# One gather of 8 KB rows per slot, into one ring of eight places, for the expert retrieval of a two-layer backbone

## The reference

```
q = (xc @ w_q).reshape(-1, 8, 2, 128)
s = einsum('chpq,hpnq->chpn', q, sub_keys)
s_top, i_top = top_k(s, 16)
cand = s_top[:, :, 0, :, None] + s_top[:, :, 1, None, :]      # 16 x 16 sums per head
best, j = top_k(cand, 16)
e = i_top[:, :, 0][j // 16] * 128 + i_top[:, :, 1][j % 16]     # one of 16384 experts
gate = softmax(best)
u = take(u_tab, e);  hid = gelu(einsum('cd,chkd->chk', xc, u))
vsel = take(v_tab, e)
out = einsum('chk,chkd->cd', gate * hid, vsel)
```

## Time and profile before

| | before |
|---|---|
| median of 3 runs | 9257.01 us |
| profiled execution, span | 9253.9 us |
| granted TensorE clock, mean | 0.894 of full speed |
| PE, DVE, ACT, POOL busy over the span | 79%, 50%, 19%, 35% |
| bytes of the gathers (queue 0) | 1342.34 MB in 368640 packets |
| gathers, U and V | 1280 and 1280 |
| median from issue to landing, U and V | 6.1 us, 6.2 us |

### The profile page before, as it was taken

How to read it: one execution, slowest core, us unless ns; L and a number is a source line. 1 busy time by engine, 2 the same in 40 slices (tenths; PEclk the granted TensorE clock), 3 DMA queues, 4 the chain that set the end, 5 groups by cost and what they waited for, 6 DMA issues and landing times. The chain is left out here.

```text
span 9253.9 us, 95340 instructions
## 1 busy us (share of the span) xinstructions
PE 7315.0 (79%) x31078; PEld 4507.4 (49%) x31078; DVE 4618.2 (50%) x10131; ACT 1801.1 (19%) x3910; POOL 3234.3 (35%) x3073
## 2 busy tenths in 40 slices
PE   6888888889867676776678888889898677666766
PEld 2777776745433222222237777777454322222322
DVE  1555544550375555555525554555304755555555
ACT  1232222210111111111112222221101111111111
POOL 0001001100027777777601100101000377777775
PEclk8999998999988888888889999999998888888888
DMA  3000000112139999999830000001111499999997
GB/s 136 16 9 9 9 9 10 30 35 60 42 107 372 349 366 352 350 363 347 317 131 9 9 9 9 13 14 30 39 52 49 171 367 349 347 357 346 368 336 283
DMA packets 627068, 1521.21 MB, mean 164 GB/s; under 512 B 56546, under 2 KB 285560, under 8 KB 626808
## 3 DMA queue, kind: packets, MB, share of 16 engines
q0 software_dynamic: 368640, 1342.34, 39.0%
q1 hardware_dynamic: 257600, 174.74, 6.2%
q10 hardware_dynamic: 568, 0.22, 0.0%
HBM read 1513.43 MB, written 3.67 MB: 164 GB/s over the span
## 5 line engine op out<-in xcount | busy, mean ns | idle before, releaser
L1793 PE MATMUL ps<-arena 128*128 128x512 f32 x5120 | 2622.3, 671 | 1118.9 <-ACT arena L1686 1116.8
L1793 PEld LDWEIGHTS ps<-arena 128*128 128x128 f32 x5120 | 1075.0, 215 | 2667.7 <-ACT arena L1686 1356.4
L1732 DVE CUSTOM_DVE_ANT_0 arena<-arena 128x1024 f32<-128x1024 f32 x1280 | 1555.5, 1227 | 1314.6 <-DMA arena<-peer_u,arena 1295.0
L424 PE MATMUL ps<-h,w 128*128 128x512 f32 x5056 | 1474.9, 452 | 310.0 <-issue 131.1
L1667 POOL DMA_INDIRECT arena<-peer_v,arena x1280 | 1437.9, 1123 | 417.9 <-issue 339.7
L1667 POOL DMA_INDIRECT arena<-peer_u,arena x1280 | 1373.8, 1073 | 514.6 <-issue 329.3
L424 PEld LDWEIGHTS ps<-h,w 128*128 128x128 f32 x5056 | 811.9, 199 | 966.4 <-issue 903.1
L690 POOL MEMSET arena<- 64x640 f32 (+1 forms) x80 | 44.7, 559 | 1853.0 <-POOLq L83 1849.4
L1764 ACT ACTIVATE arena<-arena 128x4 f32<-128x4 f32 x320 | 66.1, 207 | 2949.1 <-DVEq L1737 2949.1
L966 DVE TENSOR_TENSOR arena<-ps,level 128x512 f32<-128x512 f32 (+1 forms) x480 | 273.3, 601 | 478.6 <-PE ps L757 476.2
L763 PE MATMUL ps<-arena 128*128 128x128 f32 x3200 | 409.4, 285 | 51.9 <-DVE arena L966 51.9
(11 more groups left out here) (288 smaller groups left out, 8761.6 us busy)
## 6 DMA issues: line engine op xcount, KB each, us to landing
w<-w_in SPq DMA_DIRECT2D x132, 512.0 KB, 4.0
arena<-ada_w SPq DMA_DIRECT2D x24, 2048.0 KB, 12.2
arena<-peer_u,arena POOLq DMA_INDIRECT x1280, 6.1
arena<-peer_v,arena POOLq DMA_INDIRECT x1280, 6.2
w<-peer_wq SPq DMA_DIRECT2D x32, 512.0 KB, 6.6
w<-w_a_out SPq DMA_DIRECT2D x16, 512.0 KB, 3.6
w<-w_out SPq DMA_DIRECT2D x16, 512.0 KB, 3.8
w<-w_b_out SPq DMA_DIRECT2D x16, 256.0 KB, 2.6
```

The lines of the kernel that those rows point to most:

```text
L424: mm = eng.matmul(psum[:, c0:c0 + n], m.w[:, slot, k, :], src[:, k, c0:c0 + n], start=(k == 0), stop=(k == KB - 1))
L1732: eng.tensor_tensor_reduce(ub[:, r, :], ub[:, r, :], hs, 1.0, 0.0, ALU.mult, ALU.add, hid[:, i:i + 1]).then_inc(u_free, 1)
L1793: mm = eng.matmul(m.bank(j), dg[:, r, :], vb[:, r, 512 * j:512 * j + 512], start=False, stop=False)
```

## The change

U and V of all experts are put beside each other into one table `peer_uv` before the launch: a row holds an expert's U and V, 2048 numbers, 8 KB. One gather per slot (1 MB) fetches both. The two rings of eight places of 4 KB become one ring of eight places of 8 KB, so the memory is the same. A place is freed by the slot's matmul, through one semaphore, `freed`. U's sum no longer frees anything; its semaphore (now `summed_u`) only tells DVE that four sums are written. DVE and PE wait for the same landing. The order written out on POOL, with its lead of four slots for U, gives way to a plain loop over the slots, and the row numbers of half a group are copied just ahead of slots 0 and 16.

```
-    ub, vb, dg = m.take(RING, D), m.take(RING, D), m.take(RING, P)
+    uv, dg = m.take(RING, 2 * D), m.take(RING, P)
...
-    def gather(eng, g, i, free, table, buf, landed):
-        off = bass.IndirectOffsetOnAxis(ap=stage.bitcast(U32)[:, i % GROUP:i % GROUP + 1], axis=0)
-        eng.wait_ge(free, g * GROUP + (i + 1))
+    def gather(eng, g, i):
+        if i % HALF == 0:
+            stage_rows(eng, g, i // HALF)
+        off = bass.IndirectOffsetOnAxis(ap=stage.bitcast(U32)[:, i:i + 1], axis=0)
+        eng.wait_ge(freed, g * GROUP + (i + 1))
         eng.sem_inc(asked, 1)
-        eng.indirect_dma_start(buf[:, i % RING, :], None, table, off).then_inc(landed[i % RING], 16)
...
+        eng.indirect_dma_start(uv[:, i % RING, :], None, table, off).then_inc(uv_in[i % RING], 16)
...
-            stage_rows(eng, 0, 0)
-            for i in range(LEAD):
-                gather_u(eng, 0, i)
-            with eng.Fori(0, TILES * GROUPS_T - 1) as g:
+            with eng.Fori(0, TILES * GROUPS_T) as g:
                 for i in range(GROUP):
-                    if i == HALF - LEAD:
-                        stage_rows(eng, g, 1)
-                    if i == GROUP - LEAD:
-                        stage_rows(eng, g + 1, 0)
-                    gather_u(eng, g, i + LEAD)
-                    gather_v(eng, g, i)
...
+                    gather(eng, g, i)
...
-                        eng.wait_ge(u_in[r], before + g * (16 * (GROUP // RING)) + 16 * (i // RING + 1))
-                        eng.tensor_tensor_reduce(ub[:, r, :], ub[:, r, :], hs, 1.0, 0.0, ALU.mult, ALU.add,
-                                                 hid[:, i:i + 1]).then_inc(u_free, 1)
+                        eng.wait_ge(uv_in[r], before + g * (16 * (GROUP // RING)) + 16 * (i // RING + 1))
+                        eng.tensor_tensor_reduce(uv[:, r, 0:D], uv[:, r, 0:D], hs, 1.0, 0.0, ALU.mult, ALU.add,
+                                                 hid[:, i:i + 1]).then_inc(summed_u, 1)
...
-            eng.sem_inc(v_free, RING)
+            eng.sem_inc(freed, RING)
...
-                            mm = eng.matmul(m.bank(j), dg[:, r, :], vb[:, r, 512 * j:512 * j + 512], start=False, stop=False)
-                        mm.then_inc(v_free, 1)
+                            mm = eng.matmul(m.bank(j), dg[:, r, :], uv[:, r, D + 512 * j:D + 512 * j + 512], start=False, stop=False)
+                        mm.then_inc(freed, 1)
...
+    inputs["peer_uv"] = np.concatenate([inputs.pop("peer_u"), inputs.pop("peer_v")], axis=2)
```

More of the change, by code:

```diff
@@ L116, in __init__ @@
         self.used = 0
-        self.u_in = [ctx.enter_context(nc.semaphore(f"u_landed{i}")) for i in range(RING)]
-        self.v_in = [ctx.enter_context(nc.semaphore(f"v_landed{i}")) for i in range(RING)]
+        self.uv_in = [ctx.enter_context(nc.semaphore(f"uv_landed{i}")) for i in range(RING)]
         self.qkv_in = [ctx.enter_context(nc.semaphore(f"rwkv_weights{i}")) for i in range(3)]
@@ L1633, in stage_retrieve @@
     QS = GROUP // SUB
-    LEAD = 4
     HALF = GROUP // 2
-    u_in, v_in = m.u_in, m.v_in
+    uv_in = m.uv_in
     before = l * (16 * TILES * SLOTS // RING)
-    u_free, v_free, hid_done, gel_done, w_done, dg_done, staged, g_in = (
-        s(n) for n in ("u_free", "v_free", "hid_done", "gelu_done", "weights_done", "diag_done", "staged", "gates_in"))
+    summed_u, freed, hid_done, gel_done, w_done, dg_done, staged, g_in = (
+        s(n) for n in ("u_summed", "freed", "hid_done", "gelu_done", "weights_done", "diag_done", "staged", "gates_in"))
     dve, pair, shifted, exped, selected = (s(n) for n in ("dve", "pair", "shifted", "exponentials", "selected"))
@@ L1646, in stage_retrieve @@
     hs, sm = m.take(D), m.take(D)
-    ub, vb, dg = m.take(RING, D), m.take(RING, D), m.take(RING, P)
+    uv, dg = m.take(RING, 2 * D), m.take(RING, P)
     stage, hid, gel, wgt, g16 = (m.take(GROUP) for _ in range(5))
     gt, zero = m.take(KB), m.take(512)
-    ut = d["peer_u"].rearrange("l e c -> (l e) c")
-    vt = d["peer_v"].rearrange("l e c -> (l e) c")
+    table = d["peer_uv"].rearrange("l e c -> (l e) c")
     rows = m.ya[:, :, :].rearrange("p a b -> p (a b)").rearrange("p (t c) -> p t c", c=D)
@@ L1661, in stage_rows @@
         eng.wait_ge(staged, g * 2 + (half + 1))
-    def gather(eng, g, i, free, table, buf, landed):
-        off = bass.IndirectOffsetOnAxis(ap=stage.bitcast(U32)[:, i % GROUP:i % GROUP + 1], axis=0)
-        eng.wait_ge(free, g * GROUP + (i + 1))
-        eng.sem_inc(asked, 1)
-        eng.indirect_dma_start(buf[:, i % RING, :], None, table, off).then_inc(landed[i % RING], 16)
[L1669 to L1673, removed]
+    def gather(eng, g, i):
[3 more added lines that the diff above has]
+        eng.wait_ge(freed, g * GROUP + (i + 1))
+        eng.sem_inc(asked, 1)
+        eng.indirect_dma_start(uv[:, i % RING, :], None, table, off).then_inc(uv_in[i % RING], 16)
     def weights(eng, g, q):
@@ L1684, in diag @@
         for i in range(SUB * q, SUB * q + SUB):
-            eng.wait_ge(v_free, g * GROUP + (i + 1))
+            eng.wait_ge(freed, g * GROUP + (i + 1))
             eng.activation(dg[:, i % RING, :], m.ident[:, :], ACT.Copy, scale=wgt[:, i:i + 1]).then_inc(dg_done, 1)
@@ L1712, in _ @@
             eng.sem_inc(selected, GROUPS_T)
-            eng.sem_inc(u_free, RING)
             eng.sem_inc(x_out, 1)
@@ L1730, in _ @@
                         r = i % RING
-                        eng.wait_ge(u_in[r], before + g * (16 * (GROUP // RING)) + 16 * (i // RING + 1))
-                        eng.tensor_tensor_reduce(ub[:, r, :], ub[:, r, :], hs, 1.0, 0.0, ALU.mult, ALU.add,
-                                                 hid[:, i:i + 1]).then_inc(u_free, 1)
+                        eng.wait_ge(uv_in[r], before + g * (16 * (GROUP // RING)) + 16 * (i // RING + 1))
+                        eng.tensor_tensor_reduce(uv[:, r, 0:D], uv[:, r, 0:D], hs, 1.0, 0.0, ALU.mult, ALU.add,
+                                                 hid[:, i:i + 1]).then_inc(summed_u, 1)
                         if i % SUB == SUB - 1:
                             q = i // SUB
-                            eng.wait_ge(u_free, g * GROUP + (RING + i + 1))
+                            eng.wait_ge(summed_u, g * GROUP + (i + 1))
                             eng.sem_inc(hid_done, 1)
@@ L1789, in _ @@
                         r = i % RING
-                        eng.wait_ge(v_in[r], before + g * (16 * (GROUP // RING)) + 16 * (i // RING + 1))
+                        eng.wait_ge(uv_in[r], before + g * (16 * (GROUP // RING)) + 16 * (i // RING + 1))
                         eng.wait_ge(dg_done, g * GROUP + (i + 1))
                         for j in range(2):
-                            mm = eng.matmul(m.bank(j), dg[:, r, :], vb[:, r, 512 * j:512 * j + 512], start=False, stop=False)
-                        mm.then_inc(v_free, 1)
+                            mm = eng.matmul(m.bank(j), dg[:, r, :], uv[:, r, D + 512 * j:D + 512 * j + 512], start=False, stop=False)
+                        mm.then_inc(freed, 1)
                 for i in range(2):
```

## The result

The changed kernel takes 11872.5 us (median; 11869.4 to 11880.5), against 9263.3 us for the kernel before on the same chip: 1.2818 times its time, 95% interval 1.28 to 1.2836. It is slower by 28%.

The account below looks back on a forecast made before the run. POOL's issuing and the transfers, side by side and nearly even, were taken to bound the kernel. Two layers of 3036 us make 6072; less 3807.8 this adds 2264, and 9253.9 + 2264 + 3 gives 11,520 us, range 11,000 to 12,200.

Parts of the forecast that it names:

- last U sum to first matmul: Mid-group turn: U sum, GELU, weights and diagonal run in a row, 2.2 us.
- first matmul to first gather: Mid-group turn: from the first matmul to the next gather on POOL, 4.33 us, seen once in the earlier trace.
- first gather to its landing: Mid-group turn: 4.1 us for 512 KB plus 1.3 us for 0.52 MB more at 400 GB/s, 5.4 us.
- three further landings: Mid-group turn: transfers of slots two to four join, 3 x 2.62 = 7.9 us.
- one turn: Cycle of a mid-group subgroup, from its last U sum to the next one's: 19.8 us, against 11.9 before.
- two subgroups at a group's edge: Both last subgroups get weights at once and eight places come free in a row: 11.9 + 7 x 2.62 = 30.3 us.
- two subgroups at a tile's edge: Sums go to x first: 2.2 + 15.6 + 9.3 + 12.2 = 39.3 us, later than the transfers.
- first group of a layer: Start of a layer's retrieve stage: 5.4 + 18.3 = 23.7 us.
- the row of 123 GB/s: First microsecond after an empty queue; supported the rival of gathers each paying its own way, 13,160 us, chance 0.05.
- Two of the signs: In the changed profile: gathers land 5 to 6 us after issue; POOL waits 10 to 14 us at the matmul line.
- The costs put at nothing: Retrieve stage: 8 KB gathers on POOL, wider-row sums, halved gathers and semaphores change nothing; everything outside the stage stays.
- The faster rival: Retrieve stage: POOL's pace was the limit and is halved, transfers run without a break; about 8,800 us, chance 0.03.

Follow-up runs that it names:

- the ring of four: Changed kernel with subgroups of two slots, weights formed at once and four places in place of eight: 10665.8 us, ratio 1.155.
- the kernels with a looser order: Changed kernel with weights formed at once (0.9821), subgroups of two (0.9861), both together (0.9461), or subgroups of one (0.9497).
- the twin kernels with both orders: Changed kernel with subgroups of two and weights formed at once: one 8 KB gather per place 8740.1 us, two 4 KB gathers 9201.2 us.
- the added matmuls: Changed kernel plus twelve matmuls of zeros into an unused bank behind each of a group's first six subgroups: 11467.8 us, ratio 1.2389.
- subgroups of two with the lag: Changed kernel with subgroups of two slots, weights still formed after the next subgroup's U sums: 9134.0 us, ratio 0.9861.

## Why the prediction was right

It gave 11520 us, range 11000 to 12200; 11872.5 was measured: the change cost 2609 us where 2264 were forecast. The mechanism was the one forecast: the earlier trace rows against the groups after shows POOL's release moving from "issue" to the matmul line, and the ring of four and the kernels with a looser order show that places in flight decide.

The terms, beside the means over all 240 turns in the middle of a group and over the edges, worked out from the starts in the timeline of the changed kernel:

| term | forecast, us | measured, us |
|---|---|---|
| last U sum to first matmul | 2.2 | 2.20 |
| first matmul to first gather | 4.33 | 4.52 |
| first gather to its landing | 5.4 | 5.65 |
| three further landings | 7.9 | 8.78 |
| one turn | 19.8 | 21.14 |
| two subgroups at a group's edge | 30.3 | 31.15 |
| two subgroups at a tile's edge | 39.3 | 39.65 |
| first group of a layer | 23.7 | 24.0 |

The mis-sized term is the transfers. 240 x 1.34 = 322 us, 30 x 0.85 = 26 us and 8 x 0.35 = 3 us make 351 us, and the forecast was 352 us short. I took the rate of windows with a full queue for a queue that starts empty at every turn; the row of 123 GB/s stood in the same group, and I used it only for a rival. The 1.13 us missed per turn in the two transfer terms are 1.13 x 240 = 271 us. Most of it lies in the second landing of a turn, 3.34 us behind the first where 2.62 were forecast; the third took 2.93 and the fourth 2.51. The other 0.2 us a turn is the wait behind the first matmul, taken from a single place.

Two of the signs named in the prediction missed. The four gathers of a turn land 5.6, 6.9, 8.0 and 8.7 us after their issue, not 5 to 6 us, which holds for the first alone; the median over all is 7.9. POOL waits 14.5 us at the matmul line in the median, above the 10 to 14 named. The mean rate, 209 GB/s, is a little under the 220. The DMA share near 0.99 that the prediction reads for the kernel before is 0.95 and 0.94 in the earlier trace rows; its sum does not use it. And POOL's issuing and the transfers were not nearly even there: the twin kernels with both orders show that POOL's pace was the limit.

The costs put at nothing held: the gather of 8 KB rows has a median of 0.936 us on POOL and a mean of 1.01 (the bound of twice that is out), the U sums took 1227 ns as before, the halved gathers bought nothing in this order (11857.3 us with two gathers), and nothing changed outside of the stage. That TensorE would start each batch at the lower clock was right: the added matmuls moved the wait to the gather from 4.5 to 2.8 us and the time by 405 us, where 486 had been worked out for 270 batches; in the 210 batches that began fast, 1.8 us each are 378.

The faster rival's price, 8800 us, came near to what the one gather is worth (8740 us) in an order that keeps six gathers in flight when the last U sum starts. A gather in flight at that moment, which the prediction names against the rival, is not enough: with two the kernel took 10665.8 us, with four 9096.5 and 9134.0. By the Trainium skill, "DMA: Bandwidth & Descriptors", section "Anatomy of one DMA — SWDGE (gpsimd) path", a transfer has a constant of about 2.0 us beside bytes at 436 GB/s. The trace agrees in the sum: the shortest from issue to landing is now 5.3 us for 1 MB; less POOL's 0.94 and an estimated 2.4 for 1.05 MB at that page's 436 GB/s, 2.0 remain. It does not agree in the parts: in the mean of the 240 turns the first data move 1.65 us after the gather's start, and from there to the end of this gather's data are some 3.6 us and not 2.4. That constant alone was no reason for the gain seen: with transfers in flight it is covered, and what the halved count saves is POOL's issuing.

Two things stay open. Why a batch on an empty queue starts at 145 GB/s, and dips again after its first gather, is shown as a fact and not explained. And the difference between subgroups of two with the lag (0.986) and without it (0.946) goes with four and six gathers in flight, but was not taken apart further.

## What to carry to other kernels

When two buffers are merged into one, the joint place lives as long as the longer of the two uses; count, at the moment when the last item of a batch lands, how many places are still in flight, and compare their transfer time with the whole chain from landing to free place to next landing. If nothing is in flight, the chain is paid in every batch, whatever the transfer gained. Here batches of one, or batches of two with the weights formed at once, turned the same merge from 28% slower into 5% faster without any more memory; either step that left four gathers in flight stopped at 1 to 2% faster.

## What was not expected of the hardware

A row of 8 KB moves as one packet of 8 KB: the gathers' packets halved from 368640 to 184320 at the same bytes, and a full queue ran as fast as before, 421 GB/s in the mean over 100 us. POOL's cost of a gather did not depend on the row's length (median 0.936 us for 8 KB, 0.939 for the U rows of 4 KB). After an empty queue, the first microsecond moved only 145 GB/s in the mean over 240 turns (75 to 196). A gather beside which VectorE ran nothing took POOL at most 0.97 us in the kernel before; one that met a U sum took up to 2.0, and the gathers that met one took 1.13 in the mean.
